# Two-block float32 transformer on one core: the attention loop of the mix phase keeps masked scores and exponentials in their PSUM bank

## The reference

```
s = einsum('bqhd,bkhd->bhqk', qi, k) * scale          # 4 heads, 4 blocks of 128 query rows
s = where(causal, s, finfo.min)
p = softmax(s, axis=-1)
o = einsum('bhqk,bkhd->bqhd', p, v)
```

## Time and profile before

| what | value |
|---|---|
| time, median of 3 runs | 2682.83 us (2680.92 to 2685.48) |
| the profiled execution's own time | 2676.74 us |
| its span, first to last instruction | 2674.9 us |
| PE busy | 2597.0 us, 97% |
| POOL busy | 1629.8 us, 61% |
| DVE busy | 1168.0 us, 44% |
| ACT busy | 501.5 us, 19% |
| attention loop, first layer | from about 99 us to 148 us |
| attention loop, second layer | from about 641.6 us to 691 us |

### The profile page before, as it was taken

How to read it: one execution, slowest core, us unless ns; L and a number is a source line. 1 busy time by engine, 2 the same in 40 slices (tenths; PEclk the granted TensorE clock), 3 DMA queues, 4 the chain that set the end, 5 groups by cost and what they waited for, 6 DMA issues and landing times.

```text
span 2674.9 us, 31571 instructions
## 1 busy us (share of the span) xinstructions
PE 2597.0 (97%) x11906; PEld 2135.2 (80%) x11906; DVE 1168.0 (44%) x1664; ACT 501.5 (19%) x849; POOL 1629.8 (61%) x1113
## 2 busy tenths in 40 slices
PE   7989999999899999999999999999999999999997
PEld 6768888887688888888888888888788878888885
DVE  5844443037544440454531514882467155604325
ACT  3442111034421110201100103200400144100022
POOL 4626766665266676666766766676257615767763
PEclk9999999999899999999999999999999999999998
DMA  4112222231022222222222223222112202222221
GB/s 154 60 36 94 94 94 100 104 117 48 32 95 96 100 102 94 95 95 95 102 101 104 94 95 104 95 94 95 48 63 94 95 32 87 94 94 94 95 96 62
DMA packets 36892, 236.71 MB, mean 88 GB/s; under 512 B 4048, under 2 KB 5584, under 8 KB 9168
## 3 DMA queue, kind: packets, MB, share of 16 engines
q1 hardware_dynamic: 33456, 230.78, 24.6%
q10 hardware_dynamic: 3360, 4.85, 0.6%
HBM read 233.51 MB, written 2.10 MB: 88 GB/s over the span
## 4 chain that ended last, share of the span: by engine, by line
PE 93%; DVE 3%; ACT 1%; issue 1%; POOL 0%; DMA 0%; DVEq 0%; SPq 0%; POOLq 0%; ACTq 0%
PE psum L469 29%; PE psum L470 29%; PE psum L471 29%; PE psum L924 2%; PE psum L908 1%; PE psum L933 1%; PE psum L680 1%; DVE work L1341 1%; PE psum L809 0%; PE psum L793 0%; PE psum L499 0%; DMA x_res<-in_x 0%; POOL w_low L411 0%; PE psum L754 0%; DVE work L1695 0%
## 5 line engine op out<-in xcount | busy, mean ns | idle before, releaser
L411 POOL TENSOR_TENSOR w_low<-w_stage,w_high 128x512 fp32r<-128x512 f32 x864 | 1184.8, 1402 | 18.0
L407 POOL TENSOR_SCALAR w_high<-w_stage 128x2048 fp32r<-128x2048 f32 x216 | 415.7, 1924 | 985.6 <-PE psum L471 973.7
L469 PE MATMUL psum<-x_high,w_high 128*128 128x512 f32 x1664 | 655.4, 394 | 16.8 <-DVE x_low L1357 16.7
L470 PE MATMUL psum<-x_low,w_high 128*128 128x512 f32 x1664 | 648.6, 390 | 0.0
L471 PE MATMUL psum<-x_high,w_low 128*128 128x512 f32 x1664 | 648.6, 390 | 0.0
L469 PEld LDWEIGHTS psum<-x_high,w_high 128*128 128x128 f32 x1664 | 313.0, 188 | 85.1 <-issue 17.6
L470 PEld LDWEIGHTS psum<-x_low,w_high 128*128 128x128 f32 x1664 | 313.0, 188 | 67.2 <-issue 2.6
L471 PEld LDWEIGHTS psum<-x_high,w_low 128*128 128x128 f32 x1664 | 312.9, 188 | 65.3
L1398 DVE TENSOR_TENSOR psum<-psum,x_res 128x512 f32<-128x512 f32 x56 | 39.2, 700 | 432.7 <-PE psum L471 429.7
L469 PE MATMUL psum<-mlp_high,w_high 128*128 (+1 forms) x576 | 224.1, 389 | 0.0
L470 PE MATMUL psum<-mlp_low,w_high 128*128 (+1 forms) x576 | 224.1, 389 | 0.0
(11 more groups left out here) (268 smaller groups left out, 3463.0 us busy)
## 6 DMA issues: line engine op xcount, KB each, us to landing
w_stage<-in_wstream SPq DMA_DIRECT2D x216, 1024.0 KB, 4.9
x_res<-in_x SPq DMA_DIRECT2D x2, 1024.0 KB, 11.8
out_x<-attn_out SPq DMA_DIRECT2D x8, 256.0 KB, 2.1
inv_count_sb<-in_inv_count ACTq DMA_DIRECT2D x2, 512.0 KB, 8.6
ple_proj<-in_p ACTq DMA_DIRECT2D x2, 512.0 KB, 3.7
qk<-in_mask ACTq DMA_DIRECT2D x1, 576.0 KB, 3.7
w_spat<-in_spatial ACTq DMA_DIRECT2D x2, 256.0 KB, 5.3
diag_sb<-in_diag ACTq DMA_DIRECT2D x2, 256.0 KB, 9.2
```

The costliest lines, as they stand in the source:

```text
L407: pool.tensor_scalar(wh[:, s, :], stage[:, s, :], 1.0, 1.0, ALU.mult, ALU.mult).then_inc(high_written, 1)
L411: last = pool.tensor_tensor(wl[:, s, part], stage[:, s, part], wh[:, s, part].bitcast(F32), ALU.subtract)
L469: pe.matmul(out, wa, ra, start=start, stop=False)
L470: pe.matmul(out, wa, rb, start=False, stop=False)
```

## The change

Masked scores and exponentials stay in the scores' own PSUM bank. L1695 writes back into the bank, the exponential on ACT runs in place in the bank, and the scaling on DVE reads the bank and writes its result to the slot in `W`. The bank is released to PE only after the scaling, by a separate increment for which DVE first waits for the scaling to be complete. The wait on `probs_turned` moves from in front of L1695 to in front of the scaling.

```
@@ ACT
-  act.activation(W[:, t % 3, 0:n], W[:, t % 3, 0:n], ACT.Exp, scale=nar[:, 184 + t:185 + t],
+  act.activation(ps[:, 4 + t % 2, 0:n], ps[:, 4 + t % 2, 0:n], ACT.Exp, scale=nar[:, 184 + t:185 + t],
@@ DVE
   dve.wait_ge(scores_done, L * steps + t + 1)
-  if t >= 3:
-      dve.wait_ge(probs_turned, L * steps + t - 2)
   mx = stat[:, 20 + t % 2:21 + t % 2]
-  dve.tensor_tensor_reduce(out=W[:, t % 3, 0:n], in0=ps[:, 4 + t % 2, 0:n], in1=diag[:, T - n:T], scale=1.0,
-                           scalar=-3e38, op0=ALU.add, op1=ALU.max, accum_out=mx).then_inc(drained[4 + t % 2], 1)
-  dve.wait_ge(drained[4 + t % 2], d[4 + t % 2] + 3 + t // 2 + 1)
+  step(dve.tensor_tensor_reduce(out=ps[:, 4 + t % 2, 0:n], in0=ps[:, 4 + t % 2, 0:n], in1=diag[:, T - n:T],
+                                scale=1.0, scalar=-3e38, op0=ALU.add, op1=ALU.max, accum_out=mx))
...
   step(dve.reciprocal(stat[:, 22 + q % 2:23 + q % 2], stat[:, 3 + q % 3:4 + q % 3]))
-  dve.tensor_scalar(W[:, q % 3, 0:n], W[:, q % 3, 0:n], stat[:, 22 + q % 2:23 + q % 2], None, ALU.mult) \
+  if q >= 3:
+      dve.wait_ge(probs_turned, L * steps + q - 2)
+  dve.tensor_scalar(W[:, q % 3, 0:n], ps[:, 4 + q % 2, 0:n], stat[:, 22 + q % 2:23 + q % 2], None, ALU.mult) \
       .then_inc(probs_ready, 1)
+  dve.wait_ge(probs_ready, L * steps + q + 1)
+  dve.sem_inc(drained[4 + q % 2], 1)
```

## The result

The changed kernel takes 2692.59 us (median of 8 runs, 2689.63 to 2695.6), the kernel before beside it 2682.11 (8 runs, 2675.34 to 2685.48). The ratio is 1.0043, with a 95% interval of 1.0033 to 1.0052: slower, by 10.5 us (0.4%) where the prediction had 6.8. The time lies inside the stated range of 2683.0 to 2694.5. The profiled execution took 2690.55 us for a span of 2688.7.

The account below looks back on a forecast made before the run. PE, busy for 97% of the span, was taken to bound the kernel. Terms 0.64 + 1.27 + 1.51 = 3.42 us per layer, 6.8 for both, added to the median 2682.83, gave 2689.6 us; range 2683.0 to 2694.5.

Parts of the forecast that it names:

- Place 2: Step 11: scores wait for the scaling of step 9, so the masking starts later; cost 1.27 us per layer.
- place 3: Steps 13 and 14: scores wait for the scalings of steps 11 and 12; cost 1.51 us per layer.
- place 1: Step 6, beside POOL: scores wait for the scaling of step 4, delaying `values(0)`; cost 0.64 us per layer.
- L1698 of step 5 still ends with L407: Steps 4 to 6: POOL still holds DVE's one-column instruction until 112.71; the scaling of step 4 starts 0.71 us later.
- The rival called the clock: PE also runs at 1.2 GHz over `values(0)`: 4.8 us more for both layers, 2694.4 us; chance 0.12.
- The lock goes, and that wins: Scalings no longer held by POOL, bank wait hidden: 6.8 us less, 2676.0 us; chance 0.06.
- The early slot: L1698 of step 5 starts before POOL's L407; halfway, 1.2 us per layer less than the sum, 2687.2 us; chance 0.15.
- Hidden after the loop: Norms behind the loop take in half the delay or more: 0 to +3.4 us, 2682.8 to 2686.2; chance 0.10.

Follow-up runs that it names:

- wait_alone: Against the kernel before: only the release of the scores' bank moved behind the scaling, all data staying in SBUF; 2696.11 us, ratio 1.0058.
- release_after_exp: Against the kernel before: masking writes to the bank, exponential writes to `W`, ACT then releases the bank, scaling stays in `W`; 2685.74 us, ratio 1.0013.
- change_from_step_8: Against the changed kernel: change kept in steps 8 to 15 only, steps 0 to 7 releasing the bank right behind the masking; 2690.84 us, one run.
- after_again: The changed kernel run again with no edit, for a second profile; 2690.86 us, ratio 1.0042.

## Why the prediction was right in sign and short in size

**The mechanism** was as predicted. PE waits for DVE's release, longest in steps 11 and 13, and no masking follows right behind a scaling. `wait_alone` and `release_after_exp` show that the wait on the bank makes the loss of places 2 and 3 and the PSUM operands don't, and `change_from_step_8` that nearly all of it arises there. For the 0.5 us of place 1 this is not shown: scores 7 are also 0.2 and 0.4 us late in `change_from_step_8` and 0.49 in the second loop of `release_after_exp`, where PE waits for no bank. The moved wait on `probs_turned` cost nothing that any row shows.

**The loops.** 3.42 us per layer were predicted. Against the means of the profiles (before 64.87 where the clock stayed up in front of the first loop, and 65.05 in the second; after 68.84 and 68.76) the measured loss is 4.0 and 3.7, 7.7 us for both. Against the mean of all five profiles of before in the first loop (65.34) it is 3.5. The upper bound of the sum was 3.85 per layer, so 4.0 is just outside it. The terms were further off than the sum: place 3 was put 0.6 us too low, and 0.5 us came back behind it that nobody had counted. That these two nearly cancel is luck.

*Place 1*, predicted 0.64: scores 7 were 0.80, 0.60 and 0.66 late in the first layer and 0.48, 0.23 and 0.34 in the second, on average 0.52. The step of it that failed is "L1698 of step 5 still ends with L407". That instruction started at 115.49, when L407 was already over, and took 0.40 us; in the six loops of the changed kernel it took 0.16 to 0.40. In POOL's timeline L407 ends at 113.26:

```profile
111.35 1.91 POOL L407 TENSOR_SCALAR w_high<-w_stage 128x2048 fp32r<-128x2048 f32 x1 [0.40 <-POOL pool_in L449]
```

In part that is POOL being earlier in this loop, as above. But in `after_again` the first loop starts at 99.33, and L407 lies in it as in the kernel before, from 11.96 to 13.86 us behind the first scores (11.98 to 13.88 before):

```profile
111.29 1.90 POOL L407 TENSOR_SCALAR w_high<-w_stage 128x2048 fp32r<-128x2048 f32 x1 [0.41 <-POOL pool_in L449]
...
112.61 0.43 DVE L1693 CUSTOM_DVE_ANT_0 psum<-psum,diag_sb 128x256 f32<-128x256 f32 x1 [0.85 <-PE psum L809]
...
113.14 0.16 DVE L1695 SCALAR_TENSOR_TENSOR stat<-stat,token_cols 128x1 f32<-128x1 f32 x1
```

The masking of step 5 comes 13.28 us behind the first scores where it was 11.78, and the one-column instruction starts just as L407 ends and isn't held. The prediction had only a delay "of a few tenths" for scores 3, 4 and 5 and nothing for step 2. In fact PE waits for the release in the early steps too, and scores 5 are 2.1 to 2.6 us late in the six loops. The hold that is gone gives most of that back. So 0.52 lies near 0.64 by luck: the chain that the sum stood for isn't the one that ran.

*Place 2*, predicted 1.27, measured 1.50 (1.47 or 1.48 in each of the six loops, counted from scores 10 to the masking of step 11). From the start of the scaling to the start of the masking the trace has 134.37 to 136.14, 1.77 us: 0.48 for the scaling, 0.12 for the release, 1.12 for the scores and 0.05. The prediction had 0.42 + 0.10 + 1.02 = 1.54. The scores were the largest part of the error, 0.10 of 0.23: starting after an idle stretch, the same pair of 512-column matmuls takes 1.12 us and not 1.02.

*Place 3*, predicted 1.51, is the term that was mis-sized: measured 2.14 (4.44 less 2.30 in the table of delays; 2.07 on average over six loops, counted between scores 12 and scores 14). It splits into three. 0.21 arise before the scaling of step 11 starts, where the prediction had nothing: scores 12, which now wait 0.40 us, take 0.77 us and not 0.63, and the accumulator read behind the masking of step 12 takes 0.14 and not 0.08. 1.71 lie from there to the masking of step 13 (0.75 + 0.11 + 1.22 + 0.04, less the 0.41 of before), predicted as 1.44; the scores at half clock take 1.22 and not 1.06. The last 0.22 were predicted as 0.07.

*Given back.* Behind place 3 0.5 us return, which the prediction didn't have. `values(2)` takes 3.41 us instead of 4.07, since it starts later against the half-clock stretch, which ends at 149.4 (in the kernel before at 143.2, with `values(2)` from 139.72 on). So here the clock took less and not more. The stretch itself is 10.2 us long in both profiles.

**The operations.** The scaling from PSUM was put at the masking's lengths; it takes 60 ns more at every width (351 against 290, 751 against 690), and 0.751 us at 512 columns lies outside the bounds of 0.49 and 0.70. The slope was right: 1.04 ns per column, for 1.05. The Trainium skill (VectorE: DVE Perf Modes, Why PSUM operands drop a tier) gives a float32 operation with a PSUM operand one element per cycle, half the rate that one tensor in SBUF can reach. The trace agrees, with 1.04 ns per column against the 0.52 of SBUF. The masking's accumulator read, 141 ns against 82, was not priced at all. The exponential in PSUM takes 750 ns against 814 at 512 columns, 64 less, where the bound was 50. The release was 0.11 to 0.12 us up to PE's start, for 0.10.

**Behind the loops** nothing was hidden and nothing lost: the rest of the span is the same within 0.6 us in all profiles of the two kernels.

**The other 3.1 us.** 7.7 from the loops and 3.1 from the half-clock stretch in front of the second loop make 10.8; the medians differ by 10.5. The rival called the clock ("If it also ran at 1.2 GHz", 4.8 us) had the right kind of cause, at the wrong place and for more than the 3.1 us measured: `values(0)` ran at full clock, and unchanged code ahead of the second loop did not. That it accounts for the rest of the median rests on three profiles out of three, and on the shortest of the 14 runs.

**The rivals.** The lock goes, and that wins: no, although the held time of the scalings did go, all of it. On DVE the group fell by 4.7 us in the whole span, while PE's scores waited 6.4 us for the release in the first loop alone. But given the wait, the PSUM operands are what kept the loss at 3.8 us per layer instead of 8, as `wait_alone` beside the changed kernel shows. The early slot: in none of the six loops did the one-column instruction of step 5 get in front of L407; it started when L407 was over or within 0.05 us of its end, was held little or not at all, and scores 7 were still 0.5 late. Hidden after the loop: no, by the table of pieces.

## What to carry to other kernels

Before a buffer's release is moved later, look for the steps in which the consumer is the late engine: there, and only there, the producer's early start is what keeps the chain short, and each such step pays release, producer and restart in a row. An average of who waits for whom hides them, since ten of sixteen waits here pointed the other way. If the consumer is loaded, take work from it (14 of the 16 scalings on ACT made each loop 3 us shorter), and look what is queued behind the new work on the engine that gets it. And look for the gain in the loop as well as in the whole time: about half of these 6 us was lost again to PE's clock elsewhere.

## What the runs showed of the hardware

- A float32 scaling out of PSUM takes 351, 484, 618 and 751 ns for 128 to 512 columns, in every run alike, beside POOL or not; the same in SBUF takes 290 to 490 unheld and up to 1.54 us beside a POOL instruction. The Trainium skill (GPSIMD Engine Reference, Specifications) says that GpSimd's SBUF interfaces are shared with VectorE and contend with a DVE instruction in a two-port mode or with two SBUF inputs; these lengths agree with it.
- The read of DVE's accumulator takes 141 ns behind a masking that writes to PSUM (also 139 in `release_after_exp`) and 82 or 83 behind one that writes to SBUF.
- The exponential with its row sum takes 750 ns for 512 columns within PSUM, 777 from PSUM to SBUF and 814 within SBUF.
- PE's first matmul pair after a wait takes some 0.10 us longer than in a busy stream: 1.12 against 1.02, and 0.91 against 0.81 for 384 columns (the pair at 117.06 and that at 111.23 in the earlier trace rows).
- PE was granted 1.2 GHz for 3.4, 6.8 or 10.2 us in code in which it was busy all the time, projections with one-column sums between them, at one place in some profiles of either kernel and at another in every profile of one kernel and none of the other. A stretch of 6.8 us costs 3 us, nearly as much as what the change did to a whole loop; one of 3.4 us costs 1.6.
- Such a stretch in front of a loop also shifts POOL's work against PE's, and with it which DVE instruction is held: the same loop of the same kernel took 64.8 to 66.4 us.
